# Issuing the expert token lists and row gathers three experts ahead in a two-layer diffusion backbone with a 64-expert MoE

## The chip, the cores and the metric

The kernel runs on one core of one Trainium2 chip. The metric is the device time in microseconds (us) of one execution. Everything is in float32.

## The reference, cut to what matters

Two layers work on a latent stream of 256 tokens and a context of 256 tokens, each 1024 wide. A layer has a mixer (retention, latent attention and gated MLP branches, merged by gates) and then a mixture of experts: a router gives each token 6 of 64 experts, each expert is a SwiGLU of width 256, and one shared expert is added. Layer 0 sends all 512 tokens through its experts, layer 1 only the 256 latent tokens. For one expert e, with `idx` the tokens that chose it and `w` their routing weights, the reference computes

```
xb = t[tok_b]                                   # gather of rows
hb = silu(xb @ wg[e]) * (xb @ wu[e])            # 1024 -> 256
yb = (hb @ wd[e]).astype(float32) * w_b[:, None]  # 256 -> 1024
acc = acc.at[tok_b].add(yb)
```

On average an expert has 48 tokens in layer 0 (512 x 6 / 64) and 24 in layer 1.

## The kernel before, in words

Everything outside the expert loop is a fixed list of steps (`layer_steps`, lines 146 to 183) whose products rotate through the eight PSUM banks. Its last steps of a layer prepare the experts: `pos` and `cnt` (positions of the tokens within each expert's list, and counts), two `list` steps for experts 0 and 1, and the shared expert's down projection `sd`.

The expert loop is written by hand, once for each engine, in bodies of three experts (`three_experts`; e is the expert, j = e mod 3 its buffer). The first body is unrolled, the others are a hardware loop, and expert 63 ends after it. The capacity `cap` of a list is 128 rows in layer 0 and 64 in layer 1. In every iteration e:

- **SyncE** (lines 628 to 648) loads the three 1 MB weight matrices of expert e+3 into the slots of expert e: gate and up when gate_up(e) is done (`gu_full`), down when down(e) is done (`down_full`). So weights are held for three experts.
- **TensorE** (lines 1084 to 1094) does, in this order: `make_list(e+2)`, a product of one-hot `pick` columns with a table, which gives for each row of the list its token, its output slot and its weight, written to bank 7, columns 256 to 258; `turn_rows(e+1)`, eight transposes of the gathered rows into banks 0 and 1, after a wait on the gather (`rows_in`); a wait until VectorE has read the list of e+2 (line 1090); `turn_hidden(e-1)` into bank 7; `gate_up(e)` into bank 4+j; `down(e-1)` into banks 2 and 3. With 64 tokens or fewer, gate and up are computed side by side in halves of 64 rows (lines 1044 and 1045); with more, one after the other over all rows (lines 1051 and 1052). Line 670 holds the transposes.
- **VectorE** (lines 1882 to 1892) does `list_of(e+2)` (lines 1795 and 1796: token and slot to `idx`, weight to `wrow`), `turned(e+1)` (line 1854, copies half of the transposed rows), `hidden_turned(e-1)` (line 1870), `pick_for(e+3)` (line 1791), `hidden(e)` and `rows_down(e-1)` (line 1876). `hidden(e)` first waits until the scatter of expert e-3 has landed (`rows_out[j]`), copies the scatter index to a third column of `idx` (line 1859), and then waits for ScalarE's silu (line 1397) and multiplies with `wrow` (line 1863).
- **ScalarE** copies the other half of the transposed rows, computes the silu of the gate product, and copies the other half of the down product.
- **GpSimd** (lines 1981 to 1990) issues two indirect DMAs in order: after the list of e+2 is read, `gather(e+2)` (line 1956) of that expert's rows from `h2_rows` in DRAM into `x_rows`; after both halves of the down product of e-1 are copied, `scatter(e-1)` (line 1962) of its output rows to DRAM. Before each it loads the expert's token count and branches on it (`few`, line 548).

The queue of GpSimd's indirect DMAs and SyncE's queue of weight loads share the same 16 DMA engines.

The order of the DVE body is set by these lines:

```
list_of(e + 2, (j + 2) % 3)
turned(e + 1, (j + 1) % 3)
if j or i is not FIRST:
    hidden_turned(e - 1, (j + 2) % 3)
pick_for(e + 3, j)
hidden(e, j, i)
if j or i is not FIRST:
    rows_down(e - 1, (j + 2) % 3)
```

Of the kernel before, what the change touches and what calls it, by code (L numbers as in the profile page):

```python
# [27 lines left out]
P = 128  # L28
# [24 lines left out]
NS = 9  # L53
SLOT = 2048
BODY = 3
CAP = [128, 64]
BIG = 8192.0
PE_ROWS = 4
# [87 lines left out]
def layer_steps(l):  # L146

    mt = main_tiles(l)
    out = []
    latents = [[("c", j, t) for j in range(3) if j or t in mt] + [("cnorm", t)] for t in range(TT)]  # L150

    heads = [[("turn_c", t)] + [("turn_qk", t - 1)] * (t > 0) + [("project", t)] for t in range(TT)]
    if l == 0:
        ada = ada_steps(0, list(range(4)))
        out += [("vec",)] + ada[:2] + [("x", 0), ("x", 1)] + ada[2:4] + [("x", 2), ("x", 3), ("ms1", 0)] + ada[4:6]
        out += [("ms1", 1)] + ada[6:] + [("norm", 0), ("norm", 1)]
    else:
        out += [("comb", l - 1, 0), ("comb", l - 1, 1), ("ms1", 0), ("norm", 0)]
        out += [("comb", l - 1, 2), ("comb", l - 1, 3), ("ms1", 1), ("norm", 1)]
    out += latents[0] + latents[1] + heads[0] + latents[2] + heads[1] + latents[3]  # L160

    bulk = [("ws",)] + [("u", g) for g in range(4)] + [("gv", j, t) for j in range(2) for t in mt]
    n = len(bulk)
    out += bulk[:n // 3] + heads[2] + bulk[n // 3:2 * n // 3] + heads[3] + bulk[2 * n // 3:] + [("turn_qk", TT - 1)]
    out += [("gnorm",)]

    att = [("att", n) for n in range(len(att_units(l)) + 2)]
    bulk = [("merge", m, 2) for m in range(8)]
    if l == 0:
        bulk = weave(ada_steps(0, list(range(4, 12))), bulk)  # L170
    out += att[:4] + [("sv", t) for t in mt] + spread(att[4:], bulk)

    out += [("decay", 0)] + [("q", h) for h in range(4)] + [("decay", 1)] + [("k", h) for h in range(4)]
    out += [("v", j, t) for j in range(2) for t in range(TT)] + [("g", h) for h in range(4)]
    bulk = [("merge", m, 1) for m in range(8)]
    if l + 1 < DEPTH:
        bulk = weave(ada_steps(l + 1, list(range(12))), bulk)
    out += spread([("ret", n) for n in range(len(ret_units(l)) + 2)], bulk)
    out += [("merge", m, 0) for m in range(8)]
    out += [("out", m) for m in range(8)] + [("ms2",), ("norm", 2), ("rt",)] + [("h2", t) for t in mt]  # L180
    out += [("sg", m) for m in range(2)] + [("pos",), ("cnt",)] + [("su", m) for m in range(2)]
    out += [("list", e) for e in range(2)] + [("sd", m) for m in range(8)]
    return out


# [73 lines left out]
def backbone(nc, dram, out):  # L259
# [29 lines left out]
    with ExitStack() as ctx:  # L289
# [21 lines left out]
        eps_col = sb("eps_col", [P, 3])  # L311
        idx = sb("idx", [P, 3, 3], I32)
        wrow = sb("wrow", [P, 3])
        maxcnt = sb("maxcnt", [P, 2], I32)
        counts = sb("counts", [P, N_EXP + 2], I32)
        AREA = 22016
        area = sb("area", [P, AREA])
        bank = [ctx.enter_context(nc.psum_tensor(f"bank{i}", [P, 512], F32)) for i in range(8)]
# [69 lines left out]
        act_g = region(10752, 3, FF)  # L388
        hid = region(11520, 3, FF)
        hidT = region(12288, 3, 2 * P)  # L390
        pos1 = region(13056, TT, N_EXP + 2)
        table = area[:, 13320:13320 + TT * (N_EXP + 2) * 3].rearrange("p (t e c) -> p t e c", t=TT, c=3)
        R0 = 14112
        score = region(R0, TT, N_EXP)
        sel = region(R0 + 256, TT, N_EXP)
        mask = region(R0 + 512, TT, N_EXP)
# [65 lines left out]
        turned_dve = sem("turned_dve")  # L462
        gu_full = sem("gu_full")
        silu_done = sem("silu_done")
        hid_ready = sem("hid_ready")
        hidT_full = sem("hidT_full")
        hidT_ready = sem("hidT_ready")
# [70 lines left out]
            return slice(CTX * s - t0, CTX * s + CTX - t0)  # L538

        experts = BODY * (N_EXP // BODY)  # L540
        LISTS, PICKS = N_EXP + 1, N_EXP + 2
        lists_of = [len(range(j, LISTS, 3)) for j in range(3)]
        experts_of = [len(range(j, N_EXP, 3)) for j in range(3)]

# [121 lines left out]
        def _(pe):  # L666
# [52 lines left out]
            for l in range(DEPTH):  # L719
# [293 lines left out]

                def make_list(e, j):

                    pe.wait_ge(pick_ready, l * PICKS + e + 1)
                    pe.wait_ge(list_read, l * LISTS + e)
                    for i in range(nm):
                        last = mm(bank[7][0:cap, 256:259], pick[:, j, P * i:P * i + cap], entry(i, e), start=(i == 0), stop=(i == nm - 1))  # L1019
                    last.then_inc(list_full, 1)  # L1020

                def turn_rows(e, j, i):
# [8 lines left out]

                def gate_up(e, j, i):
                    gp, up = moe_at[l] + 3 * j, moe_at[l] + 3 * j + 1
                    pe.wait_ge(turned_act, l * N_EXP + e + 1)
                    pe.wait_ge(turned_dve, l * N_EXP + e + 1)
                    pe.wait_ge(piece_loaded[gp % NS], 16 * (gp // NS + 1) + 16 * i)
                    pe.wait_ge(piece_loaded[up % NS], 16 * (up // NS + 1) + 16 * i)
                    wg, wu = piece_view(gp, KT, FF), piece_view(up, KT, FF)

                    def halves():  # L1040

                        for k in range(KT):
                            x = x_rowsT[:, j, cap * k:cap * k + P // 2]
                            mm(bank[4 + j][0:P // 2, 0:FF], x, wg[:, k, :], start=(k == 0), stop=(k == KT - 1))  # L1044
                            last = mm(bank[4 + j][P // 2:P, 0:FF], x, wu[:, k, :], start=(k == 0), stop=(k == KT - 1))  # L1045
                        last.then_inc(gu_full, 1)

                    def whole():
                        for k in range(KT):
                            x = x_rowsT[:, j, cap * k:cap * k + cap]  # L1050
                            mm(bank[4 + j][:, 0:FF], x, wg[:, k, :], start=(k == 0), stop=(k == KT - 1), skip_group_check=True)  # L1051
                            last = mm(bank[4 + j][:, FF:2 * FF], x, wu[:, k, :], start=False, stop=(k == KT - 1), skip_group_check=True)  # L1052
                        last.then_inc(gu_full, 1)

                    by_size(pe, pe_passed, l, e, halves, whole)
# [28 lines left out]
                def three_experts(i):  # L1084
                    for j in range(BODY):
                        e = i * BODY + j
                        make_list(e + 2, (j + 2) % 3)
                        turn_rows(e + 1, (j + 1) % 3, i + (j + 1) // 3)
                        if j or i is not FIRST:
                            pe.wait_ge(list_read, l * LISTS + e + 3)  # L1090
                            turn_hidden(e - 1, (j + 2) % 3)
                        gate_up(e, j, i)
                        if j or i is not FIRST:
# [341 lines left out]
        def _(dve):  # L1435
# [76 lines left out]
            for l in range(DEPTH):  # L1512
# [292 lines left out]

                def step_cnt():
                    b = await_full(dve, ("cnt", l))
                    v.memset(counts[:, N_EXP:N_EXP + 2], 0)
                    v.tensor_copy(counts[:, 0:N_EXP], b[:, 0:N_EXP])
                    link(v.tensor_reduce(need[:, 0:1], b[:, 0:N_EXP], AX_X, ALU.max))  # L1810
                    dve.nop().then_inc(emptied["dve"], 1)
# [10 lines left out]
                def step_list(e):  # L1822
# [2 lines left out]
                    link(read_list(e, b[:, 0:3]))  # L1825
                    dve.nop().then_inc(list_read, 1)  # L1826
                    dve.nop().then_inc(emptied["dve"], 1)

                def step_sd(m):
                    residual(("sd", l, m), mod[:, l, 40 + m, :], m)  # L1830
# [13 lines left out]
                    picks(e, j, const_cols("iota1")[:, 0:cap]).then_inc(pick_ready, 1)  # L1844

                def list_of(e, j):
                    dve.wait_ge(list_full, l * (LISTS - 2) + e - 1)
                    if not isinstance(e, int) or e >= 3:
                        dve.wait_ge(hid_ready, l * N_EXP + e - 2)
                    read_list(j).then_inc(list_read, 1)  # L1850

                def turned(e, j):
                    dve.wait_ge(rows_turned, l * N_EXP + e + 1)
                    v.tensor_copy(x_rowsT[:, j, 4 * cap:8 * cap], bank[1][:, 0:4 * cap]).then_inc(turned_dve, 1)  # L1854

                def hidden(e, j, i):
                    dve.wait_ge(list_read, l * LISTS + e + 1)
                    dve.wait_ge(rows_out[j], 16 * l * experts_of[j] + 16 * i)
                    v.tensor_copy(idx[0:cap, j, 2:3], idx[0:cap, j, 1:2])
                    dve.wait_ge(silu_done, l * N_EXP + e + 1)  # L1860

                    def gated(m, up):
                        v.scalar_tensor_tensor(out=hid[0:m, j, :], in0=act_g[0:m, j, :], scalar=wrow[0:m, j:j + 1], in1=up,  # L1863
                                               op0=ALU.mult, op1=ALU.mult).then_inc(hid_ready, 1)

                    by_size(dve, dve_passed, l, e, lambda: gated(P // 2, bank[4 + j][P // 2:P, 0:FF]), lambda: gated(P, bank[4 + j][:, FF:2 * FF]))
# [15 lines left out]
                def three_experts(i):  # L1882
                    for j in range(BODY):
                        e = i * BODY + j
                        list_of(e + 2, (j + 2) % 3)
                        turned(e + 1, (j + 1) % 3)
                        if j or i is not FIRST:
                            hidden_turned(e - 1, (j + 2) % 3)
                        pick_for(e + 3, j)
                        hidden(e, j, i)  # L1890
                        if j or i is not FIRST:
                            rows_down(e - 1, (j + 2) % 3)
# [2 lines left out]
                with dve.Fori(1, N_EXP // BODY) as i:  # L1895
                    three_experts(i)
                hidden_turned(experts - 1, 2)
                hidden(experts, 0, N_EXP // BODY)
                rows_down(experts - 1, 2)
                hidden_turned(experts, 0)  # L1900
# [36 lines left out]
        def _(pool):  # L1937
# [4 lines left out]
            for l in range(DEPTH):  # L1942
# [31 lines left out]
                pool.wait_ge(moe_ready, l + 1)  # L1974
                for j in range(2):
                    pool.wait_ge(h2_stored[j], 16 * h2_base(l + 1, j))
                for e in range(2):
                    pool.wait_ge(list_read, l * LISTS + e + 1)
                    gather(cap, e, rows_in[e])

                def three_experts(i):
                    for j in range(BODY):
                        e = i * BODY + j
                        j2 = (j + 2) % 3
                        pool.wait_ge(list_read, l * LISTS + e + 3)
                        fitted(e + 2, gather, j2, rows_in[j2])
                        if j or i is not FIRST:
                            pool.wait_ge(y_act, l * N_EXP + e)
                            pool.wait_ge(y_dve, l * N_EXP + e)
# [54 lines left out]
```

## Time and profile before

| | |
|---|---|
| median of 3 runs | 2792.06 us (2790.34 to 2795.26) |
| profiled execution: span | 2791.2 us; no time outside the span is reported for it |
| PE busy | 2423.6 us (87%), 13062 instructions |
| DVE busy | 764.5 us (27%) |
| ACT busy | 482.0 us (17%) |
| POOL busy | 272.8 us (10%) |
| weight queue (q1) | 541.62 MB, 53.5% of 16 engines |
| indirect and other GpSimd DMAs (q0) | 61.07 MB, 6.1% |

PE is TensorE, DVE is VectorE, ACT is ScalarE, POOL is GpSimd. A busy PE is a PE with a matmul in its pipeline, at whichever clock was granted. The expert loops lie at about 880 to 1605 us (layer 0) and 2120 to 2750 us (layer 1) of the span.

### The profile page before, as it was taken

How to read it: one execution, taken by the hardware profiler on the slowest of the kernel's cores; microseconds unless marked ns; L12 is line 12 of the kernel's file. 1: busy time of each engine (PE TensorE's matmuls, PEld its weight loads, DVE VectorE, ACT ScalarE, POOL GpSimd, SP SyncE). 2: the span in 40 equal slices, each digit the busy share in tenths (PEclk: the TensorE clock that was granted, in tenths of full speed). 3: DMA queues.
4: the chain of work that ended last, by engine and by line, in shares of the span. 5: the costliest groups of instructions: out<-in, count | busy, mean ns of one | idle time of the engine just before them, and what ended most of it. 6: DMA issues, size and time to landing. Idle time of an engine off the chain costs nothing.

```text
span 2791.2 us, 39130 instructions
## 1 busy us (share of the span) xinstructions
PE 2423.6 (87%) x13062; PEld 1605.6 (58%) x13063; DVE 764.5 (27%) x2357; ACT 482.0 (17%) x1015; POOL 272.8 (10%) x320
## 2 busy tenths in 40 slices
PE   4997999999988988888888869899988778787876
PEld 3665556554455555556665567677876445444545
DVE  2324320231133323222223223431323222222221
ACT  3331111120020111111111113320221111111110
POOL 1000000000001111111111120000001111111111
PEclk9998999999989888999998889999999888888888
DMA  8132452464224888788878850432446888888884
GB/s 277 46 109 64 130 166 68 147 202 154 83 89 148 329 317 342 286 319 305 311 267 312 303 218 31 136 114 68 131 152 252 328 333 333 338 331 333 333 332 177
DMA packets 219213, 608.19 MB, mean 218 GB/s; under 512 B 22027, under 2 KB 152277, under 8 KB 169973
## 3 DMA queue, kind: packets, MB, share of 16 engines
q1 hardware_dynamic: 191584, 541.62, 53.5%
q0 software_dynamic: 26128, 61.07, 6.1%
q10 hardware_dynamic: 1412, 4.28, 0.4%
q8 instruction: 60, 0.98, 0.1%
q14 instruction: 29, 0.23, 0.0%
HBM read 596.94 MB, written 35.00 MB: 226 GB/s over the span
## 4 chain that ended last, share of the span: by engine, by line
PE 69%; DMA 15%; issue 6%; DVE 4%; POOLq 3%; ACT 2%; DVEq 1%; POOL 0%; ACTq 0%; SPq 0%
PE bank L677 25%; DMA area<-h_rows,idx 14%; PE bank L1044 11%; PE bank L685 6%; PE bank L670 6%; PE bank L1076 5%; PE bank L1051 2%; POOLq L548 2%; PE bank L1052 2%; PE bank L714 2%; PE bank L748 2%; DVE area L1876 1%; PE bank L824 1%; PE bank L802 1%; PE bank L839 1%
## 5 line engine op out<-in xcount | busy, mean ns | idle before, releaser
L1044 PE MATMUL bank<-ring,area 128*64 128x256 f32 x1840 | 530.1, 453 | 23.4 <-issue 19.9
L1045 PE MATMUL bank<-ring,area 128*64 128x256 f32 x1840 | 530.2, 453 | 0.0
L677 PE MATMUL bank<-hT,ring 128*128 128x512 f32 (+1 forms) x1408 | 481.1, 498 | 0.0
L670 PE MATMUL bank<-const,area 128*128 128x128 f32 (+3 forms) x1668 | 256.9, 301 | 227.8 <-DMA area<-h_rows,idx 183.9
L1044 PEld LDWEIGHTS bank<-ring,area 128*64 128x64 f32 x1840 | 291.8, 165 | 210.8 <-issue 125.3
L677 PEld LDWEIGHTS bank<-hT,ring 128*128 128x128 f32 x1408 | 265.6, 191 | 192.0 <-issue 176.3
L670 PEld LDWEIGHTS bank<-const,area 128*128 128x128 f32 (+3 forms) x1668 | 218.2, 189 | 266.2 <-issue 222.7
L1045 PEld LDWEIGHTS bank<-ring,area 128*64 128x64 f32 x1840 | 291.7, 165 | 0.0
L1076 PE MATMUL bank<-ring,area 128*64 128x512 f32 (+1 forms) x1024 | 267.2, 596 | 3.3 <-issue 2.5
L1956 POOL DMA_INDIRECT area<-h_rows,idx x130 | 123.6, 951 | 1425.6 <-DVEq L1826 1306.4
L677 PE MATMUL bank<-area,ring 128*128 128x512 f32 (+1 forms) x704 | 237.8, 486 | 2.8 <-issue 2.8
L1863 DVE SCALAR_TENSOR_TENSOR area<-area,wrow,bank 64x256 f32<-64x256 f32 (+1 forms) x128 | 61.7, 482 | 635.6 <-ACT area L1397 504.2
L1962 POOL DMA_INDIRECT expert_rows<-area,idx x128 | 118.1, 923 | 1034.5 <-issue 1034.5
L677 PEld LDWEIGHTS bank<-area,ring 128*128 128x128 f32 x704 | 133.4, 190 | 96.3 <-issue 87.3
L685 PE MATMUL bank<-ring,hT 128*128 128x256 f32 (+1 forms) x800 | 166.9, 370 | 6.2 <-ACT hT L1204 6.2
L685 PEld LDWEIGHTS bank<-ring,hT 128*128 128x128 f32 x800 | 147.4, 192 | 28.5 <-ACT hT L1204 6.3
L1397 ACT ACTIVATE area<-bank 128x256 f32<-128x256 f32 (+1 forms) x128 | 48.8, 381 | 645.5 <-PE bank L1045 505.4
L1173 ACT ACTIVATE area<-bank 128x512 f32<-128x512 f32 (+1 forms) x122 | 60.9, 505 | 517.5 <-PE bank L677 417.7
L1076 PEld LDWEIGHTS bank<-ring,area 128*64 128x64 f32 (+1 forms) x1024 | 84.6, 143 | 111.6 <-issue 96.9
L1854 DVE COPY area<-bank 128x512 f32<-128x512 f32 (+1 forms) x128 | 71.5, 558 | 229.7 <-PE bank L670 220.6
L1019 PEld LDWEIGHTS bank<-area 128*128 128x128 f32 (+1 forms) x756 | 86.5, 173 | 81.4 <-issue 81.2
L1393 ACT ACTIVATE area<-bank 128x512 f32<-128x512 f32 (+1 forms) x128 | 62.8, 491 | 375.9 <-PE bank L670 365.1
(192 smaller groups left out, 2039.4 us busy)
## 6 DMA issues: line engine op xcount, KB each, us to landing
ring<-in_moe_w_gate SPq DMA_DIRECT2D x128, 1024.0 KB, 7.0
ring<-in_moe_w_up SPq DMA_DIRECT2D x128, 1024.0 KB
ring<-in_moe_w_down SPq DMA_DIRECT2D x128, 1024.0 KB
ring<-in_w_in SPq DMA_DIRECT2D x52, 1024.0 KB, 7.9
ring<-in_ada_w SPq DMA_DIRECT2D x48, 1024.0 KB, 11.5
area<-expert_rows POOLq DMA_DIRECT2D x36, 512.0 KB, 7.6
ring<-in_w_out SPq DMA_DIRECT2D x8, 1024.0 KB, 9.0
ring<-in_w_br_gmlp SPq DMA_DIRECT2D x8, 512.0 KB, 8.4
```

Source lines behind the costliest of these rows:

```text
L670: return nc.tensor.transpose(dst, src, ident[0:n, 0:n])
L677: last = mm(b[:, 0:n], lhs[:, k, :], rhs[:, k, c:c + n], start=(k == 0), stop=(k == K - 1))
L685: last = mm(b[:, 0:n], lhs[:, k, P * tt:P * tt + P], rhs[:, k, :], start=(k == 0), stop=(k == K - 1))
L1019: last = mm(bank[7][0:cap, 256:259], pick[:, j, P * i:P * i + cap], entry(i, e), start=(i == 0), stop=(i == nm - 1))
L1044: mm(bank[4 + j][0:P // 2, 0:FF], x, wg[:, k, :], start=(k == 0), stop=(k == KT - 1))
L1045: last = mm(bank[4 + j][P // 2:P, 0:FF], x, wu[:, k, :], start=(k == 0), stop=(k == KT - 1))
L1076: last = mm(bank[2 + hf][o * hf:o * hf + m, :], hidT[:, j, cap * k:cap * k + m], wd[:, k, 512 * hf:512 * hf + 512], start=(k == 0), stop=( ...
L1393: af(x_rowsT[:, j, 0:4 * cap], bank[0][:, 0:4 * cap], ACT.Copy).then_inc(turned_act, 1)
L1854: v.tensor_copy(x_rowsT[:, j, 4 * cap:8 * cap], bank[1][:, 0:4 * cap]).then_inc(turned_dve, 1)
L1863: v.scalar_tensor_tensor(out=hid[0:m, j, :], in0=act_g[0:m, j, :], scalar=wrow[0:m, j:j + 1], in1=up, op0=ALU.mult, op1=ALU.mult).then_inc ...
L1956: pool.indirect_dma_start(out=x_rows[0:m, j, :], out_offset=None, in_=h2_dram[0:tokens(l), :], in_offset=bass.IndirectOffsetOnAxis(ap=idx[ ...
L1962: pool.indirect_dma_start(out=y_dram[0:TOPK * tokens(l), :], out_offset=bass.IndirectOffsetOnAxis(ap=idx[0:m, j, 2:3], axis=0), in_=y_rows ...
```

## The change

- The first `list` steps are three instead of two (`AHEAD = 3`), and the loop works on list e+3, its gather, and the pick columns of e+4. The tables have four spare experts instead of two.
- The list product goes to columns 0 to 2 of bank 4+(j+1) mod 3, the bank of gate_up(e+1), instead of bank 7. It waits until the hidden rows of expert e-2 are made; gate_up(e) now waits for the reading of list e+2, and the wait ahead of `turn_hidden` is gone.
- A new step `stage(e)` on VectorE, behind `hidden_turned(e-1)` and ahead of `list_of(e+3)`, holds the wait for the scatter of expert e-3 and the copy of the scatter index, and also copies the routing weight aside into `scale`; `hidden(e)` multiplies with `scale`.
- `list_of` stands behind `turned` and `hidden_turned` instead of ahead of them.
- GpSimd gathers for e+3 into buffer j ahead of the scatter of e-1.

```diff
-    out += [("list", e) for e in range(2)] + [("sd", m) for m in range(8)]
+    out += [("list", e) for e in range(AHEAD)] + [("sd", m) for m in range(8)]
...
-        LISTS, PICKS = N_EXP + 1, N_EXP + 2
+        LISTS, PICKS = N_EXP + AHEAD - 1, N_EXP + MORE - 1
...
                 def make_list(e, j):
 
+                    b = bank[4 + (j + 1) % 3]
                     pe.wait_ge(pick_ready, l * PICKS + e + 1)
                     pe.wait_ge(list_read, l * LISTS + e)
+                    if not isinstance(e, int) or e >= AHEAD + 2:
+                        pe.wait_ge(hid_ready, l * N_EXP + e - AHEAD - 1)
                     for i in range(nm):
-                        last = mm(bank[7][0:cap, 256:259], pick[:, j, P * i:P * i + cap], entry(i, e), start=(i == 0), stop=(i == nm - 1))
+                        last = mm(b[0:cap, 0:3], pick[:, j, P * i:P * i + cap], entry(i, e), start=(i == 0), stop=(i == nm - 1))
...
                 def gate_up(e, j, i):
+                    if not isinstance(e, int) or e:
+                        pe.wait_ge(list_read, l * LISTS + e + AHEAD)
...
-                        make_list(e + 2, (j + 2) % 3)
+                        make_list(e + AHEAD, j)
                         turn_rows(e + 1, (j + 1) % 3, i + (j + 1) // 3)
                         if j or i is not FIRST:
-                            pe.wait_ge(list_read, l * LISTS + e + 3)
                             turn_hidden(e - 1, (j + 2) % 3)
...
+                    if e == 0:
+                        picks(AHEAD, 0, const_cols("iota1")[:, 0:cap]).then_inc(pick_ready, 1)
...
                 def list_of(e, j):
-                    dve.wait_ge(list_full, l * (LISTS - 2) + e - 1)
+                    dve.wait_ge(list_full, l * (LISTS - AHEAD) + e - AHEAD + 1)
+                    dve.wait_ge(staged, l * N_EXP + e - AHEAD + 1)
+                    read_list(j, bank[4 + (j + 1) % 3][:, 0:3]).then_inc(list_read, 1)
+
+                def stage(e, j, i):
+
+                    dve.wait_ge(list_read, l * LISTS + e + 1)
+                    dve.wait_ge(rows_out[j], 16 * l * experts_of[j] + 16 * i)
                     if not isinstance(e, int) or e >= 3:
                         dve.wait_ge(hid_ready, l * N_EXP + e - 2)
-                    read_list(j).then_inc(list_read, 1)
+                    v.tensor_copy(idx[0:cap, j, 2:3], idx[0:cap, j, 1:2])
+                    v.tensor_copy(scale[0:cap, j:j + 1], wrow[0:cap, j:j + 1]).then_inc(staged, 1)
...
                 def hidden(e, j, i):
-                    dve.wait_ge(list_read, l * LISTS + e + 1)
-                    dve.wait_ge(rows_out[j], 16 * l * experts_of[j] + 16 * i)
-                    v.tensor_copy(idx[0:cap, j, 2:3], idx[0:cap, j, 1:2])
+                    dve.wait_ge(staged, l * N_EXP + e + 1)
                     dve.wait_ge(silu_done, l * N_EXP + e + 1)
...
-                        list_of(e + 2, (j + 2) % 3)
                         turned(e + 1, (j + 1) % 3)
                         if j or i is not FIRST:
                             hidden_turned(e - 1, (j + 2) % 3)
-                        pick_for(e + 3, j)
+                        stage(e, j, i)
+                        list_of(e + AHEAD, j)
+                        pick_for(e + MORE, (j + 1) % 3)
                         hidden(e, j, i)
...
-                        pool.wait_ge(list_read, l * LISTS + e + 3)
-                        fitted(e + 2, gather, j2, rows_in[j2])
+                        pool.wait_ge(list_read, l * LISTS + e + AHEAD + 1)
+                        fitted(e + AHEAD, gather, j, rows_in[j])
```

## Rows read from the trace of the kernel before

**Rows 1.** The page's chain that ended last: shares of the span by line.

```profile
PE bank L677 25%; DMA area<-h_rows,idx 14%; PE bank L1044 11%; PE bank L685 6%; PE bank L670 6%; PE bank L1076 5%; PE bank L1051 2%; POOLq L548 2%; PE bank L1052 2%; PE bank L714 2%; PE bank L748 2%; DVE area L1876 1%; PE bank L824 1%; PE bank L802 1%; PE bank L839 1%
```

**Rows 2.** Who waited for the gathers, by stage: layer 0 first, then layer 1.

```profile
  PE bank L670: 56.6, 36
...
  PE bank L670: 125.7, 30
```

**Rows 3.** Windows: both expert loops (columns in the first line).

```profile
core 0: us, PE busy (x) PEld busy (x) DVE busy (x) ACT busy (x) POOL busy (x), PEclk, DMA share, GB/s
880.00:1600.00 720.00, 629.60 (x3678) 418.16 (x3678) 206.29 (x694) 99.86 (x190) 120.18 (x126) 0.89 0.81 307
2126.00:2735.00 609.00, 481.23 (x3296) 296.46 (x3294) 147.44 (x549) 82.53 (x183) 110.49 (x122) 0.84 0.87 333
```

**Rows 4.** Chain of layer 1, 2380 to 2425 us: start, duration, what.

```profile
2390.56 0.70 DVE area L1876
...
2394.52 7.79 DMA area<-h_rows,idx
2402.44 1.35 PE bank L670 x10
...
2409.64 1.75 PE bank L1076 x8
```

**Rows 5.** Windows from one down product's end to the next: two of layer 1, three of layer 0.

```profile
2390.56:2397.43 6.87, 6.87 (x57) 4.44 (x55) 2.42 (x9) 1.35 (x3) 1.83 (x2) 1.00 0.84 313
2397.43:2411.40 13.97, 9.09 (x57) 5.36 (x55) 2.39 (x9) 1.35 (x3) 1.86 (x2) 0.76 0.85 332
1225.71:1234.26 8.55, 7.61 (x58) 5.00 (x57) 2.86 (x11) 1.58 (x3) 1.97 (x2) 1.00 0.89 320
937.43:947.70 10.27, 9.39 (x59) 5.76 (x60) 3.27 (x12) 1.58 (x3) 1.87 (x2) 0.83 0.91 346
1374.90:1387.30 12.40, 11.21 (x58) 8.47 (x59) 3.14 (x11) 1.58 (x3) 2.02 (x2) 1.00 0.83 306
```

**Rows 6.** Lines of layer 0, 880 to 1620 us: gate and up products, small and large.

```profile
L1045 PE MATMUL bank<-ring,area 128*64 128x256 f32 x816 | 231.5, 447 | 0.0
L1052 PE MATMUL bank<-ring,area 128*128 128x256 f32 x208 | 68.0, 412 | 0.0
```

**Rows 7.** Layer 0: issues of down weights (each ends a down product), and the loop's last down product.

```profile
893.73 0.33 SPq L633 DMA_DIRECT2D ring<-in_moe_w_down  x1
...
957.96 0.33 SPq L633 DMA_DIRECT2D ring<-in_moe_w_down  x1
...
968.20 0.33 SPq L633 DMA_DIRECT2D ring<-in_moe_w_down  x1
...
1464.42 0.33 SPq L633 DMA_DIRECT2D ring<-in_moe_w_down  x1
1474.94 0.33 SPq L633 DMA_DIRECT2D ring<-in_moe_w_down  x1
...
1599.52 5.31 PE bank L1076 x8
```

**Rows 8.** DVE timeline of one iteration of layer 1.

```profile
2391.29 0.15 DVE L1795 TENSOR_SCALAR idx<-bank 64x2 int32<-64x2 f32 x1
...
2392.32 0.41 DVE L1791 TENSOR_SCALAR area<-const,area 128x64 f32<-128x64 f32 x2
2392.64 0.14 DVE L1859 COPY idx<-idx 64x1 int32<-64x1 int32 x1
...
2396.13 0.48 DVE L1863 SCALAR_TENSOR_TENSOR area<-area,wrow,bank 64x256 f32<-64x256 f32 x1 [3.35 <-ACT area L1397]
```

**Rows 9.** DMA issues of layer 1's loop: down loads, count, KB each.

```profile
ring<-in_moe_w_down SPq DMA_DIRECT2D x61, 1024.0 KB
```

**Rows 10.** Landing of the scatters: layer 0 first, then layer 1.

```profile
DMA to landing us min/median/max: 5.9/6.9/8.9
...
DMA to landing us min/median/max: 5.5/6.1/8.0
```

More of the change, by code:

```diff
@@ L55 @@
 BODY = 3
+AHEAD = 3
+MORE = AHEAD + 1
 CAP = [128, 64]
@@ L313, in backbone @@
         wrow = sb("wrow", [P, 3])
+        scale = sb("scale", [P, 3])
         maxcnt = sb("maxcnt", [P, 2], I32)
-        counts = sb("counts", [P, N_EXP + 2], I32)
+        counts = sb("counts", [P, N_EXP + MORE], I32)
         AREA = 22016
@@ L390, in backbone @@
         hidT = region(12288, 3, 2 * P)
-        pos1 = region(13056, TT, N_EXP + 2)
-        table = area[:, 13320:13320 + TT * (N_EXP + 2) * 3].rearrange("p (t e c) -> p t e c", t=TT, c=3)
-        R0 = 14112
+        pos1 = region(13056, TT, N_EXP + MORE)
+        table = area[:, 13328:13328 + TT * (N_EXP + MORE) * 3].rearrange("p (t e c) -> p t e c", t=TT, c=3)
+        R0 = 14144
         score = region(R0, TT, N_EXP)
@@ L464, in backbone @@
         silu_done = sem("silu_done")
+        staged = sem("staged")
         hid_ready = sem("hid_ready")
@@ L1807, in step_cnt @@
                     b = await_full(dve, ("cnt", l))
-                    v.memset(counts[:, N_EXP:N_EXP + 2], 0)
+                    v.memset(counts[:, N_EXP:N_EXP + MORE], 0)
                     v.tensor_copy(counts[:, 0:N_EXP], b[:, 0:N_EXP])
@@ L1856, in hidden @@
                 def hidden(e, j, i):
-                    dve.wait_ge(list_read, l * LISTS + e + 1)
-                    dve.wait_ge(rows_out[j], 16 * l * experts_of[j] + 16 * i)
-                    v.tensor_copy(idx[0:cap, j, 2:3], idx[0:cap, j, 1:2])
+                    dve.wait_ge(staged, l * N_EXP + e + 1)
                     dve.wait_ge(silu_done, l * N_EXP + e + 1)
                     def gated(m, up):
-                        v.scalar_tensor_tensor(out=hid[0:m, j, :], in0=act_g[0:m, j, :], scalar=wrow[0:m, j:j + 1], in1=up,
+                        v.scalar_tensor_tensor(out=hid[0:m, j, :], in0=act_g[0:m, j, :], scalar=scale[0:m, j:j + 1], in1=up,
                                                op0=ALU.mult, op1=ALU.mult).then_inc(hid_ready, 1)
@@ L1897, in _ @@
                 hidden_turned(experts - 1, 2)
+                stage(experts, 0, N_EXP // BODY)
                 hidden(experts, 0, N_EXP // BODY)
@@ L1976, in _ @@
                     pool.wait_ge(h2_stored[j], 16 * h2_base(l + 1, j))
-                for e in range(2):
+                for e in range(AHEAD):
                     pool.wait_ge(list_read, l * LISTS + e + 1)
```

## The prediction

> **What bounds the kernel now.** I read the chain of work first. It gives 14% of the span (about 390 us) to the landing of gathers [rows 1]; nothing else that the change touches comes near. The waits put the direct price lower: TensorE's transposes sat idle for gathers 56.6 us in layer 0 and 125.7 us in layer 1 [rows 2], 182 us together. The two differ because the chain also counts the time in which other work goes on beside a gather.
>
> The chain of layer 1 then shows the loop that repeats. A down product ends at 2390.5, VectorE copies it in 0.70 us, GpSimd issues that expert's scatter and behind it a gather at 2394.5, the gather lands 7.79 us later, and only then do transposes, gate and up, and the down product run, to 2411.4 [rows 4]. One turn takes 20.85 us and covers two iterations. The windows between down products show the same from TensorE's side: a short iteration of 6.87 us at granted clock 1.00, then one of 13.97 us at 0.76 [rows 5], and so on alternately. Two iterations in 20.84 us: the loop through the gather sets the pace, at 10.4 us per expert here. Over the whole loop of layer 1 it is 609 us for 61 down loads [rows 3, 9], 10.0 us per expert.
>
> What is next late is in the same windows. The DMA engines are busy 0.87 of the layer-1 loop and 0.81 of layer 0's [rows 3]: 0.87 x 609 / 61 = 8.7 us of transfers per expert in layer 1, against 6.87 us for TensorE at full clock. In layer 0, TensorE needs 8.55 us for a small expert (1225.7 to 1234.3, clock 1.00) and 12.40 us where a large one is multiplied [rows 5].
>
> **The change, step by step.**
>
> Gather one expert earlier. The gather is issued at the same place of an iteration, behind the same scatter, but has one more iteration before `turn_rows` needs it. The old loop closed over two iterations; the new one closes over three: 0.70 + 3.26 us from the down product to the gather's issue, 7.8 us to land, 0.13 us, then 6.9 us of TensorE, 18.8 us in all [rows 4, 5], or 6.3 us per iteration. That is below both TensorE (6.87) and the transfers (8.7), so the wait goes to nothing in both layers. Bounds: the 182 us of [rows 2] at most directly, plus what slow clock the waits caused; at least what the new bound leaves.
>
> Layer 1. The bound becomes the transfers. SyncE issues down(e+3), gate and up(e+4) together when a down product ends, two iterations ahead of their use, so when TensorE waits for weights three more matrices are already queued and the queue does not run dry. 61 experts x 8.7 us = 530 us instead of 609 us: -79. The last expert is not held by a gather either: -4. TensorE will then wait about 1.8 us in each iteration, and some of it will come back as slow clock: a 13.97 us iteration holds 9.09 us of busy TensorE instead of 6.87 [rows 5], so a slow-clock iteration is slightly longer than the 8.7 us of transfers. I put +8 for it. Sum **-75 us**. Bounds: -85 (transfers alone) and, with every iteration at 9.1 us, 61 x (10.0 - 9.1) = -50.
>
> Layer 0. 51 experts are small (816 products over 16) and 13 large (208 over 16) [rows 6]. At full clock without waits the 63 intervals from 893.7 to 1604.8 [rows 7] would be 50 x 8.5 + 13 x 12.4, and 13 x 2.0 more because the interval after a large gate and up has the large down product (10.52 us, [rows 7]): 612 us. The trace has 711. Of the 99 us between, 57 are gather waits; some 42 are slow clock: the 10.27 us interval at 0.83 against 8.55 at 1.00 [rows 5] prices one slow stretch at 1.7 us, so there are about 25. The waits go, -57. Slow stretches right behind long waits go too; I take a third of 42, -14, since others stand in stretches without such a wait. The list wait ahead of `turn_hidden` gives -4. Transfers are close behind: 0.81 x 720 = 583 us for the loop [rows 3], less than TensorE's 612 on average, but in a run of small experts 0.91 x 10.27 = 9.3 us against TensorE's 8.5; for such runs I add +10. Sum **-65 us**. Bounds: -99 (everything above 612 goes) and -14: all 37 intervals between small experts and all 13 large ones pay 1.7 us, 612 + 85 = 697.
>
> The moved and added work. `stage` adds one copy of 64x1, like L1859's 0.14 us [rows 8], on a VectorE that then waits 3.35 us for the silu: hidden, 128 x 0.15 = 19 us if it were not. The list read (0.15 for its first half) and the picks (0.41) stay on VectorE, only behind the copies that TensorE waits for; hence part of the -4 above. The list products stay on TensorE at the same place; the new bank asks for the hidden rows of e-2, which `turn_hidden(e-2)` waited for an iteration before: zero. gate_up's new wait is for a list read one iteration earlier: zero. On GpSimd the number of issues per iteration is the same; one more dummy gather per layer, about 1 us, lies beside compute. One more list step ahead of each loop and three more picks ahead of the lists: under 1 us each, +2 in all for both layers.
>
> The moved wait for the scatter. `stage` now waits for the scatter of e-3 ahead of list read, picks and `hidden(e)`. That scatter is issued ahead of the gather, so less than 4 us after its down product ends, and lands in 6.1 us in layer 1, 6.9 us in layer 0, 8.9 at most [rows 10]: some 10 to 13 us after that end. `stage(e)` is reached one iteration (8.7) plus about 2 us later (L1859's place, [rows 8]), so the wait is met or nearly met, and `hidden` needs it only 3.5 us after that, at L1863's place. Zero, and a delay of the list costs nothing as long as the gather keeps its spare iteration.
>
> Sum: -75 - 65 + 2 = -138 us. The profiled execution has 2791.2 us of span and nothing listed around it, 0.9 us below the median of 2792.06, so I set the forecast against the median: 2792 - 138 = **2654 us**.
>
> **The rivals.**
>
> *A, forecast: gather waits vanish, layer 1 becomes transfer-bound, layer 0 stays with TensorE.* 2654 us, 0.66.
>
> *B: the clock gives nothing back.* For it: 10.2 to 10.3 us intervals follow one another in layer 0 (937.4 to 947.7, 958.0 to 968.2, [rows 5, 7]) with TensorE busy 9.39 of them, so the slow clock there may not be the gather's doing. Then layer 0 gains 14 and layer 1 50: 2792 - 64 = 2728. 0.13.
>
> *C: TensorE stays at full clock.* For it: the intervals at 1.00 in [rows 5]; against: weight waits remain. -99 and -85: 2792 - 184 = 2608. 0.13.
>
> *D: the gather is no quicker to arrive than it is needed.* If transfers fill the queue without a break, gathers could land later. The pace would stay at 10 us only if the new loop took three times that: 30 - 3.96 - 0.13 - 6.9 = 19 us landing against 7.8. 2792 us, 0.03.
>
> *E, slower: each iteration waits for weights and then runs at the slow clock.* Place: layer 1's gate_up. Price: 9.09 us of slow-clock work plus the 1.8 us wait is 10.9 us per expert, 0.9 more than now, +55 over 61; layer 0 gains only its lower bound, 14: 2792 + 41 = 2833. It decides from the point where slow work plus wait passes 10.0 us. Against it: the wait is the difference between transfers and TensorE's work, so work of 9.09 us leaves no wait at 8.7 us of transfers, and in [rows 5] the short iteration, which stands between two such slow ones, has the clock at 1.00 throughout. 0.05, with the scatter wait that holds `stage` until it delays `hidden` (it would need landings far above 8.9 us) in it.
>
> The Trainium skill, "TensorE: Matmul & The Clock Gate", section "HAM oscillation — how this bites in real kernels", speaks for E: it describes a kernel whose tiles each wait for a transfer and each start at the reduced clock. The trace shows such a start only behind the long gather wait of every second iteration; by the page it would be every iteration, and the time E's 2833.
>
> **How the numbers follow.** A, B and C hold 0.92. The range takes A, C and the upper half of what lies between A and B: 2605 to 2712 us; beyond it lie most of B, D, E and a gain larger than C. About 0.2% (5.6 us) is what a measurement can tell from no change. Faster by more than that: A, B, C, 0.92; within it: D, 0.03; slower: E, 0.05.
>
> **What would show it.** Right: the transposes' wait for gathers near zero in both layers; windows of layer 1 of equal length, about 8.7 to 9 us, instead of 7 and 14, with a DMA share near 1.0 and a wait of TensorE for the gate and up weights in place of the gather; layer 0's loop near 646 us, layer 1's from its first down load to its last near 535 us. Wrong: gathers that still stand in the chain (D); layer-0 intervals between small experts that stay at 10.2 us with clock 0.83 and no wait (B); DMA share below 0.95 in layer 1 while TensorE waits (another cause than the transfers).

## The result and the profile after

| | before | after |
|---|---|---|
| median | 2791.2 us (2785.84 to 2795.26, 4 runs) | 2579.32 us (2575.93 to 2583.78, 4 runs) |
| profiled span | 2791.2 us | 2574.2 us |
| granted TensorE clock, mean of the span | 0.914 | 0.95 |

The ratio is 0.9244, 95% interval 0.9222 to 0.9265: 212 us less. The forecast was 2654 us in a range of 2605 to 2712; the sign was right, the size was short by a third of what came. The measured time lies 26 us below the range.

First the wait that the change aims at. Who waited for the gathers, over the whole kernel after (us, times):

```profile
  PE bank L674: 0.9, 1
```

It was 56.6 and 125.7 us in the two loops [rows 2]. The chain that ended last, by line, names the new bound:

```profile
PE bank L681 27%; DMA ring<-in_moe_w_up 15%; PE bank L1053 10%; PE bank L689 6%; PE bank L1085 6%; PE bank L674 5%; PE bank L1060 2%; PE bank L718 2%; PE bank L1061 2%; PE bank L1026 2%; PE bank L752 2%; PE bank L828 1%; PE bank L843 1%; PE bank L806 1%; PE bank L800 1%
```

The gather's 14% [rows 1] are gone, and the loading of the up weights stands there with 15%. The windows of the expert loops after, layer 0 and layer 1, then single intervals from one down product's end to the next: one of a small expert (64 tokens or fewer) and one of a large expert in layer 0, and two of layer 1. The last three columns are the granted clock as a part of full speed, the mean busy share of the 16 DMA engines, and GB/s. The clock's records in these traces are 1.0 or 0.5, so a value between them means that TensorE ran for a part of the stretch at half speed.

```profile
core 0: us, PE busy (x) PEld busy (x) DVE busy (x) ACT busy (x) POOL busy (x), PEclk, DMA share, GB/s
880.00:1480.00 600.00, 566.55 (x3682) 380.24 (x3681) 215.89 (x760) 100.19 (x191) 119.96 (x126) 0.97 0.97 370
1995.00:2525.00 530.00, 465.71 (x3354) 318.93 (x3356) 160.66 (x624) 83.88 (x187) 113.42 (x124) 0.91 0.99 385
902.02:909.54 7.52, 7.52 (x59) 4.86 (x59) 3.61 (x13) 1.58 (x3) 1.87 (x2) 1.00 1.00 367
1228.01:1238.99 10.98, 10.98 (x60) 8.49 (x59) 3.53 (x13) 1.58 (x3) 1.88 (x2) 1.00 1.01 366
2143.61:2150.50 6.89, 6.80 (x58) 4.91 (x56) 2.57 (x10) 1.35 (x3) 1.80 (x2) 1.00 1.00 407
2150.50:2160.61 10.11, 8.49 (x58) 5.95 (x56) 2.58 (x10) 1.35 (x3) 1.80 (x2) 0.83 1.00 389
```

Three things stand in these lines. The DMA share rose from 0.81 and 0.87 [rows 3] to 0.97 and 0.99: both loops, not layer 1 alone, are now close to the pace of the transfers (e4 below tests it). TensorE's interval for a small expert of layer 0 is 7.52 us, and for a large one 10.98 us, where the intervals at full clock of before were 8.55 and 12.40 [rows 5]. Those two held gather waits of 0.21 and 0.95 us. The interval from 893.69 to 902.18 held none and still took 8.49 us: about a microsecond of it was neither gather wait nor slow clock. And the granted clock in layer 0 rose from 0.89 to 0.97.

All loops below are given from the end of their first to the end of their last down product: 711 and 618 us before, 585 and 531 us after. Layer 0 gave 126 us and layer 1 gave 87.

**The microsecond in layer 0.** TensorE's matmuls across one iteration's start, before and then after (start, duration, what, idle before):

```profile
893.62 1.05 PE L1019 MATMUL bank<-area 128*128 128x3 f32 x8
894.54 1.58 PE L670 MATMUL bank<-const,area 128*128 128x128 f32 x10
896.79 0.42 PE L1044 MATMUL bank<-ring,area 128*64 128x256 f32 x1 [0.68 <-issue]
```

```profile
901.95 1.05 PE L1026 MATMUL bank<-area 128*128 x8
902.86 1.35 PE L674 MATMUL bank<-const,area 128*128 128x128 f32 x10
904.15 0.43 PE L1053 MATMUL bank<-ring,area 128*64 128x256 f32 x1
```

The ten transposes took 1.58 us and now take 1.35; the gate product started 0.68 us behind them and now follows at once. The same stretches by the line that reads a token count (`few`: line 548 before, 552 after), on TensorE's queue: before and after.

```profile
L548 PEldq TENSOR_LOAD <-counts x1: 297/297/297, 896.0 to 896.0; - x1
```

```profile
L552 PEldq TENSOR_LOAD <-counts x1: 309/309/309, 903.1 to 903.1; - x1
```

Before, TensorE's queue stood at the wait for the list read ahead of `turn_hidden`, and read the count for gate_up's branch only at 896.0, behind it. After, nothing stops the queue there: it reads the count at 903.1, while the transposes that began at 902.86 still run, and the branch costs nothing in this iteration. The waits of before listed the gap all along, as TensorE idle for "issue", the word for time in which nothing visible was waited for (layer 0's loop; us, times, longest):

```profile
PE bank L670 <- DMA area<-h_rows,idx: 56.6, 36, 4.8
PE bank L1044 <- issue: 19.9, 31, 0.8
PE bank L1051 <- issue: 5.1, 7, 1.0
```

The gap is not gone everywhere. In 15 of 62 iterations of layer 0 the changed kernel's gate product starts over 0.3 us behind the transposes, and in 14 of them a weight matrix landed 0.2 to 0.4 us ahead of the count read: the branch is now exposed behind the wait for weights. Here the count was read only at 1039.8, 0.9 us before the product:

```profile
1040.69 0.42 PE L1053 MATMUL bank<-ring,area 128*64 128x256 f32 x1 [3.50 <-issue]
L552 PEldq TENSOR_LOAD <-counts x1: 423/423/423, 1039.8 to 1039.8; - x1
```

The longest such gap is 3.8 us, most of it the wait; no run prices the branch in them by itself.

### The profile page after: what moved, and what is told of

It is laid out like the page before. It is cut to its first block, busy times and chain, and to the rows that moved or that the text cites. A ratio compares the mean times of both kernels' runs of the same rounds, so it can differ in the third digit from the quotient of the medians.

```text
span 2574.2 us, 39493 instructions
## 1 busy us (share of the span) xinstructions
PE 2334.1 (91%) x13074; PEld 1587.1 (62%) x13075; DVE 785.2 (31%) x2495; ACT 481.7 (19%) x1015; POOL 273.9 (11%) x322
## 4 chain that ended last, share of the span: by engine, by line
PE 74%; DMA 17%; issue 3%; DVE 2%; ACT 2%; SPq 1%; ACTq 0%; DVEq 0%; POOLq 0%; POOL 0%
PE bank L681 27%; DMA ring<-in_moe_w_up 15%; PE bank L1053 10%; PE bank L689 6%; PE bank L1085 6%; PE bank L674 5%; PE bank L1060 2%; PE bank L718 2%; PE bank L1061 2%; PE bank L1026 2%; PE bank L752 2%; PE bank L828 1%; PE bank L843 1%; PE bank L806 1%; PE bank L800 1%
## 5 line engine op out<-in xcount | busy, mean ns | idle before, releaser
L1053 PE MATMUL bank<-ring,area 128*64 128x256 f32 x1840 | 477.1, 418 | 84.5 <-DMA ring<-in_moe_w_up 63.2
L1054 PE MATMUL bank<-ring,area 128*64 128x256 f32 x1840 | 478.4, 419 | 0.0
L1053 PEld LDWEIGHTS bank<-ring,area 128*64 128x64 f32 x1840 | 267.9, 151 | 221.5 <-issue 97.1
L674 PE MATMUL bank<-const,area 128*128 128x128 f32 (+3 forms) x1668 | 233.8, 282 | 41.9 <-ACT area L1312 23.2
L1054 PEld LDWEIGHTS bank<-ring,area 128*64 128x64 f32 x1840 | 267.8, 151 | 0.0
L674 PEld LDWEIGHTS bank<-const,area 128*128 128x128 f32 (+3 forms) x1668 | 207.4, 190 | 71.2 <-issue 30.9
L1879 DVE SCALAR_TENSOR_TENSOR area<-area,scale,bank 64x256 f32<-64x256 f32 (+1 forms) x128 | 61.7, 482 | 539.0 <-ACT area L1405 286.5
L1181 ACT ACTIVATE area<-bank 128x512 f32<-128x512 f32 (+1 forms) x122 | 60.9, 505 | 515.2 <-PE bank L681 417.1
L1892 DVE COPY area<-bank 64x512 f32<-64x512 f32 (+1 forms) x128 | 88.7, 693 | 126.0 <-PE bank L1085 82.5
L1658 DVE SCALAR_TENSOR_TENSOR area<-area,bank 128x512 f32<-128x512 f32 (+1 forms) x48 | 26.6, 554 | 318.3 <-PE bank L681 308.6
```

Source lines behind the costliest of these rows:

```text
L674: return nc.tensor.transpose(dst, src, ident[0:n, 0:n])
L1181: return af(dst, b[:, :] if src is None else src(b), func, **kw).then_inc(emptied["act"], 1)
L1892: v.tensor_copy(y_rows[0:m, j, 512:1024], bank[3][o:o + m, :]).then_inc(y_dve, 1)
```

## The experiments

Theory 1: the change has two gains, the gather's spare iteration in both layers, and in layer 0 the branch that is no longer exposed behind a wait; together they bring both loops to the pace of the transfers. Theory 2: all of it is the earlier gather and the quicker clock behind it. The loop times are those of the profiled execution, the totals are medians. Each kernel below is the changed one with one thing altered, except where said.

| kernel | median us | layer 0 loop | layer 1 loop | gather waits |
|---|---|---|---|---|
| before | 2791 | 711 | 618 | 184 |
| e1_two_ahead | 2782 | 699 | 619 | 218 |
| e5_gather_late | 2770 | 687 | 621 | 214 |
| e7_bank7 | 2677 | 677 | 533 | none |
| e2_wait_kept | 2610 | 622 | 533 | none |
| e3_list_first | 2585 | 586 | 533 | none |
| after | 2579 | 585 | 531 | 1 |
| after, again (e8) | 2579 | 587 | 531 | 0 |
| e4_half_down | 2476 | 552 | 467 | 0 |
| e6_no_branch | 2716 | 715 | 533 | 0 |

**e1_two_ahead: all but the distance** (the bank's index and the added first picks go back with it).

```diff
-AHEAD = 3
+AHEAD = 2
...
-                        make_list(e + AHEAD, j)
+                        make_list(e + AHEAD, (j + 2) % 3)
...
-                        list_of(e + AHEAD, j)
-                        pick_for(e + MORE, (j + 1) % 3)
+                        list_of(e + AHEAD, (j + 2) % 3)
+                        pick_for(e + MORE, j)
...
-                        fitted(e + AHEAD, gather, j, rows_in[j])
+                        fitted(e + AHEAD, gather, j2, rows_in[j2])
```

> The changed kernel with lists, picks and gathers two experts ahead again; the other bank, the removed wait, stage and the VectorE order stay. Theory 1 (two separate gains: the gather waits, and in layer 0 about 1 us per iteration because TensorE no longer stops ahead of turn_hidden and so reads the token count for gate_up's branch while the transposes run): the loop through the gather closes over two iterations again. Layer 1 goes back to about 613 us. In layer 0 intervals between small experts without a gather wait are 7.5 us, not 8.5, but part of that turns into longer gather waits: some 660 us. Total about 2735 us. Theory 2 (all comes from the earlier gather and the quicker clock behind it): layer 0 back at 711 us, its undisturbed small intervals at 8.5 us, total about 2790 us.

Measured 2782.21 us, ratio to before 0.9958 (0.9936 to 0.9981). Between the two totals, nearer theory 2's. But the interval lengths decide against theory 2: the shortest one between small experts is 7.52 us, not 8.49. TensorE did get its microsecond; it spent it waiting for gathers (us, times):

```profile
  PE bank L674: 218.3, 85
```

184 us in 67 waits became 218 in 85. So the moved wait alone is worth 9 us, since the loop through the gather, which closes over two iterations, sets the pace whatever TensorE saves. My 660 us for layer 0 was too hopeful (699): with the distance at two TensorE still waited for gathers there 90 us in 40 waits.

**e5_gather_late: only the gather's issue late.** GpSimd issues the scatter of e-1 first.

```diff
-                        pool.wait_ge(list_read, l * LISTS + e + AHEAD + 1)
-                        fitted(e + AHEAD, gather, j, rows_in[j])
                         if j or i is not FIRST:
                             pool.wait_ge(y_act, l * N_EXP + e)
                             pool.wait_ge(y_dve, l * N_EXP + e)
                             fitted(e - 1, scatter, j2, rows_out[j2])
+                        pool.wait_ge(list_read, l * LISTS + e + AHEAD + 1)
+                        fitted(e + AHEAD, gather, j, rows_in[j])
```

> The changed kernel with GpSimd's order swapped: the scatter of e-1 is issued ahead of the gather of e+3, so the gather is issued about one iteration later, as late before its use as in the kernel before, while lists, picks and bank stay as changed. If the gather's spare iteration is what pays: gather waits of 180 us or more come back, layer 1 near 613 us, layer 0 near 660 us, total about 2735 us, as with two ahead. If the earlier lists or the other order pay: within 20 us of 2579 us.

Measured 2770.25 us, ratio 0.993 (0.9903 to 0.9958), gather waits 213.8 us in 69 waits. Lists, picks and bank three ahead, and nearly nothing gained: it is the gather's issue time that counts, not the list's. Swapping two entries of one engine's queue takes back 191 of the 212 us.

**e7_bank7: the distance**, with the list product in bank 7, TensorE's wait ahead of `turn_hidden`, and VectorE's list read ahead of its copies, as before. It isn't quite the distance alone: `stage`, which the kernel before does not have, stands ahead of the list read.

```diff
-                    b = bank[4 + (j + 1) % 3]
+                    b = bank[7][:, 256:259]
...
-                    if not isinstance(e, int) or e:
-                        pe.wait_ge(list_read, l * LISTS + e + AHEAD)
...
                         if j or i is not FIRST:
+                            pe.wait_ge(list_read, l * LISTS + e + AHEAD + 1)
                             turn_hidden(e - 1, (j + 2) % 3)
...
+                        stage(e, j, i)
+                        list_of(e + AHEAD, j)
                         turned(e + 1, (j + 1) % 3)
                         if j or i is not FIRST:
                             hidden_turned(e - 1, (j + 2) % 3)
-                        stage(e, j, i)
-                        list_of(e + AHEAD, j)
```

> Only the distance changes: lists and gathers three ahead, but the list product in bank 7, TensorE's wait for its reading ahead of turn_hidden, and VectorE reading the list first, as in the kernel before; stage is needed and stands ahead of the list read. Theory: the gather waits go (-181 us as in e2), the exposed branch stays, and the scatter wait now holds TensorE too: from a down product over scatter, stage and list to the down product two iterations later 3.3 + 6.9 + 0.6 + 6.5 = 17.3 us, 8.6 per iteration, just above the 8.4 of e2. Total 2610 to 2645 us. If the bank and order were worth nothing: 2579 us.

Measured 2676.53 us, ratio 0.9586 (0.9561 to 0.961): above the expected range, by 32 us. Layer 1 has its whole gain (533 us) and layer 0 a quarter of it (677 us). TensorE now stands idle ahead of the two transposes of `turn_hidden` for the weight column of the list, which VectorE writes late (one start of an iteration in layer 0, then all such waits of that loop: us, times, longest):

```profile
955.96 1.12 PE L674 MATMUL bank<-const,area 128*128 128x128 f32 x8
957.67 0.48 PE L674 MATMUL bank<-const,area 128*128 128x128 f32 x2 [0.59 <-DVE wrow L1801]
```

```profile
PE bank L674 <- DVE wrow L1801: 33.7, 61, 2.0
```

In the kernel before that wait was 1.3 us in 4 waits. What stands ahead of the list read now and did not before is `stage`: in layer 0 the weight column is written 2.18 us (median) after the down product's end, against 1.81 us before, and VectorE waited 12 us for scatters in `stage` there.

Transposes with that wait take 2.11 us on average in layer 0's intervals of small experts against 1.38 after, the branch gap of 0.73 us comes behind it, and the clock is granted at 0.95 there against 0.98. With e1 this makes a square: the distance without the moved wait gives 115 us, the moved wait without the distance 9, both 212. The 97 us between e7 and the changed kernel is not the price of the old wait as it stood: it holds the late list as well, which neither the kernel before nor the changed one has.

**e2_wait_kept: a wait of like place put back**, on VectorE's copy of the down rows, behind which the list read of before stood. The list is not waited for here.

```diff
                         if j or i is not FIRST:
+                            if not isinstance(e, int) or e >= 2:
+                                pe.wait_ge(y_dve, l * N_EXP + e - 1)
                             turn_hidden(e - 1, (j + 2) % 3)
```

> The changed kernel with a wait put back ahead of turn_hidden, on VectorE's copy of the down rows of expert e-2, which stands in VectorE's queue where the list read of before stood. Gathers stay three ahead. Theory 1: in layer 0 gate_up starts 0.7 us after the transposes again, small intervals go from 7.5 to about 8.4 us, the loop from 585 to 620-640 us; in layer 1, which has no branch, an interval gains at most 0.15 us and the transfers hide it. Total 2615 to 2635 us. Theory 2 (earlier gather and clock alone): within 10 us of 2579 us.

Measured 2609.74 us, ratio 0.9347 (0.9319 to 0.9375), layer 0 at 622 us, layer 1 unchanged within 3 us. As theory 1 said, a little below its range of totals; theory 2's 2579 is out. The transposes take only 0.07 us longer, but gate_up starts late again:

```profile
911.22 1.42 PE L674 MATMUL bank<-const,area 128*128 128x128 f32 x10
913.54 0.42 PE L1053 MATMUL bank<-ring,area 128*64 128x256 f32 x1 [0.90 <-ACT area L1403]
```

Put back like this, the wait costs 30 us of the total, and 37 us in layer 0's loop of the profiled execution (which was the slowest of four). This is the nearest that the runs come to the price of the old wait.

ScalarE is named as releaser because its copy ended last before; gate_up needs no copy of that iteration, and layer 1, with the same copies and no branch, shows no cost.

**e6_no_branch: e2's wait, without the branch behind it.** Layer 0's gate and up, and VectorE's `hidden`, always take the form for large experts; e2's wait, not shown here, is in.

```diff
-                    by_size(pe, pe_passed, l, e, halves, whole)
+                    whole() if cap == P else halves()
```

> As e2_wait_kept (wait ahead of turn_hidden), but in layer 0 gate_up and hidden always take the form for large experts, without reading the token count and branching. If the branch behind the wait is what costs the time: gate_up follows the transposes without a gap (e2 had 0.89 us on average), intervals are about 10.9 us for all, and the total is about 2710 us from the larger products. If the wait itself costs it: a gap of 0.8 to 0.9 us stays and the total is about 2765 us.

Measured 2716.39 us, ratio 0.9713 (0.9691 to 0.9736): 6 us from the first expectation, 49 from the second. TensorE's idle time between transposes and gate product is 0.00 us over layer 0 (they overlap by about 0.15 us in the pipeline) where e2 had a gap of 0.89 on average, with the very same wait. So it is the count read and branch behind a wait that cost the time, and the wait alone costs nearly nothing. The clock is granted at 1.00 over this loop, the DMA share is 0.82:

```profile
900.00:1610.00 710.00, 705.71 (x3580) 544.79 (x3581) 210.42 (x739) 97.52 (x186) 117.26 (x123) 1.00 0.82 308
```

**e3_list_first: VectorE's order put back alone.**

```diff
+                        stage(e, j, i)
+                        list_of(e + AHEAD, j)
                         turned(e + 1, (j + 1) % 3)
                         if j or i is not FIRST:
                             hidden_turned(e - 1, (j + 2) % 3)
-                        stage(e, j, i)
-                        list_of(e + AHEAD, j)
```

> The changed kernel with VectorE's order put back: stage and list_of ahead of the copies of transposed rows and transposed hidden rows. If the order is worth nothing (gate_up needs the rows copied an iteration later, and transfers set the pace): within 15 us of 2579. If the scatter wait in stage then holds VectorE ahead of the copy of the transposed hidden rows, which the down product needs: scatters land some 10 us after their down product, stage would stand 1.6 us into the third iteration after it (about 7.5 + 1.6 us in a run of small experts at full clock), so up to 1 us per iteration in layer 0, part of it hidden by the transfers: 2590 to 2630 us.

Measured 2584.76 us, ratio 0.925 (0.9229 to 0.9271), against 0.9232 (0.9213 to 0.9251) for the changed kernel on the same chip. The intervals overlap; the medians are 5 us apart, so the order is worth 0.2% at most once TensorE doesn't wait for the list. VectorE did wait for scatters in `stage`, 81 us in 56 waits over both loops, and nearly none of it reached the total.

**e8_after_again.** The control for the last group.

> The changed kernel itself on the same chip as these three, so that differences of some 10 us among them can be read: 2570 to 2590 us under every theory.

Measured 2579.32 us (2577.12 to 2582.07).

**e4_half_down: less to transfer.** In the loop only half of each down matrix is loaded.

```diff
-                    sp.dma_start(slot_of(p), expert_src(l, kind, e)).then_inc(piece_loaded[p % NS], 16)
+                    part = SLOT // 2 if kind == 2 else SLOT
+                    sp.dma_start(slot_of(p)[:, 0:part], expert_src(l, kind, e)[:, 0:part]).then_inc(piece_loaded[p % NS], 16)
```

> The changed kernel with only half of each down matrix loaded inside the loop (the other half of the slot keeps old weights, so the output differs); 0.52 MB or about 1.36 us of transfers less per expert, TensorE's work unchanged. If transfers set the pace in both layers: layer 1 from 531 to about 445 us (TensorE's 6.8 us per expert plus a few waits), layer 0 from 585 to about 550 us, total about 2460 us. If TensorE and its clock set the pace: above 2560 us.

Measured 2476.14 us, ratio 0.8872 (0.8847 to 0.8896). Layer 0 is at 552 us as expected, layer 1 at 467 instead of 445. With TensorE's instructions unchanged, 103 us went with the bytes, so the transfers do set the pace after. In layer 1 they still nearly do here (windows of the two loops):

```profile
895.00:1440.00 545.00, 533.94 (x3579) 361.11 (x3578) 211.62 (x739) 97.39 (x186) 117.42 (x123) 1.00 0.93 342
1970.00:2425.00 455.00, 429.87 (x3268) 289.36 (x3266) 157.38 (x602) 81.97 (x182) 111.13 (x121) 0.95 0.98 371
```

Layer 1 fell 22 us short of the expectation: the DMA share is still 0.98 and TensorE is busy for 430 of 455 us, so both are close to binding there, and no run separates them. In layer 0 TensorE takes over at full clock, which is the remaining floor of that loop, some 550 us.

No run points to a kernel faster than the changed one with the same work: it moves the same bytes at a DMA share of 0.97 to 0.99, and every other alteration that leaves the work as it is was slower or equal.

## Why the prediction was wrong in size

**Right.** "The loop through the gather sets the pace", closing over two iterations before and three after: the waits went from 182 us to 1, and e1 and e5 bring them back by undoing just that. "The bound becomes the transfers" in layer 1: forecast -75, measured -87; 0.99 x 530 us of busy DMA engines for 61 experts is 8.6 us each against my 8.7. The scatter wait in `stage`, put at zero: in e3, with `stage` ahead of the copies, it costs 5 us at most. That holds only while TensorE doesn't wait for the list; in e7 the same `stage` delays the list and TensorE with it. The added copy and picks were put at hidden; no run prices them alone.

**Wrong, and the step that failed.** "The list wait ahead of `turn_hidden` gives -4." That is 0.06 us in each of 63 iterations, and the prediction gives no working for it. e2, which puts a like wait back, prices it at 30 us of the total and 37 us in layer 0's loop; layer 1 differs by 2. Even the transposes alone were stretched by 0.2 us. Left out was what stands behind the wait in TensorE's own queue: the read of the token count (0.30 us) and the branch, 0.7 to 0.9 us together. They are free while TensorE still has transposes to run, and exposed behind a wait (e2 against e6). Layer 1 has no such branch, and its 6.87 us interval shrank only to some 6.8.

**The floor that followed from it.** "612 us" for layer 0 at full clock "without waits" was summed from 8.5 and 12.4 us intervals. The first holds the exposed branch. The 12.40 us interval was not free of waits: TensorE is idle for 1.19 of it, and 0.95 of that is a gather wait:

```profile
1376.61 1.37 PE L670 MATMUL bank<-const,area 128*128 128x128 f32 x10 [0.95 <-DMA area<-h_rows,idx]
```

With 7.5 and 11.0 and 1.9 for a large down product, the same sum is 50 x 7.5 + 13 x 11.0 + 13 x 1.9 = 543 us; e4, with less to transfer, reached 552. The lower bound of -99 rested on 612, so the range ended at 2605. With 543 us for TensorE and my own 583 us for the transfers of that loop [rows 3], the transfers are the later of the two, and 585 us came. By this estimate TensorE's floor is 69 us lower without the exposed branch; 37 of them show against e2, since the transfers bind before it is reached.

**The clock.** I gave back a third of layer 0's 42 us of slow clock and took 10 for weight waits, and charged layer 1 with 8. This was the second term of layer 0 that was mis-sized. Without the list wait's 4 us my terms give 711 - 57 - 14 + 10 = 650 us for that loop; e2, which keeps an exposed branch, is at 622. So about 28 of the 61 us by which layer 0 came out lower are here and about 33 in the list wait. The trace shows 38 of 62 intervals below full clock before, where I had put about 25. After, and in e2, there are 9; e1, with gather waits and no exposed branch, has 31. The slow stretches went with the gather waits, most of them and not a third. In layer 1 slow stretches stay (granted 0.91), but they fall into time that the transfers take anyway: the 10.11 us interval shown above is at 0.83 and its neighbour lasts 6.89 us, 8.5 on average. Rival E, and with it the rule of the Trainium skill, "TensorE: Matmul & The Clock Gate", section "HAM oscillation — how this bites in real kernels", that a kernel whose tiles wait for a transfer starts each of them at the reduced clock, is seen here in 25 of 62 intervals of layer 1 and not in every one. The loop takes 531 us with a DMA share of 0.99, so the slow clock shows next to nothing in its time.

**Rivals.** C was nearest (2608), and in part by luck. In layer 0 TensorE is near full clock, as C says, but it has 99 us there where 126 came, since it leaves out the branch. Its 85 us for layer 1 fit the 87, though the clock there stayed at 0.91. B, D and E are out. The lower gain of layer 1 that B uses has a slip: 61 x (10.0 - 9.1) is 55, not 50.

## What to carry to other kernels

Price a wait by what stands behind it in its own engine's queue, register loads and branches above all, not by the stretch of the instruction that it releases; idle time put down to "issue" behind a wait is the sign, and a stage without the branch is the wrong place to read the price. Where a loop closes over n iterations through a transfer, ask for one more iteration of lead before anything else: until then what the engines save is only waited away (9 us alone, 30 us or more on top). And sum a floor for each resource separately, from intervals whose every idle gap has been looked at, before taking the highest one.

## What was not expected of the hardware

I had kept a rival (D) for gathers that land later once the weight queue never runs dry. Layer 1 shows no such thing. From issue to landing of the gathers in its loop after (min, median, max), at a DMA share of 0.99:

```profile
DMA to landing us min/median/max: 5.6/6.5/8.1
```

The chain of before had 7.79 us for one at a share of 0.87 [rows 3, 4]; the 31 that TensorE waited for in that loop took 7.05 us (median). In layer 0 it is open: 7.9 us (median) and 10.7 at most after, and before 7.2 and 9.3 for the 36 that were waited for, with no figure for the others. Nor did I expect TensorE's clock to be granted at 1.00 throughout in e6, whose loop of layer 0 has longer products and no gap ahead of them, where the kernel before had 0.89.
